# Feed-forwards of a two-block transformer: the third gate/up piece computed by seven block products, like the pieces behind it

## The chip, the cores and the metric

One core of a Trainium2 chip runs the whole program as one kernel launch. Its engines are named as the profile names them: PE multiplies matrices (PEld is its loading of weights), DVE and ACT work elementwise, POOL issues some loads and does a few copies, SP issues the other loads. The metric is the device time of one execution in microseconds; less is better.

## The reference

A first block (mixer and a mixture of experts) is followed by two layers of a second block. Each of these layers has two gated feed-forwards with a mixer between them, so there are four feed-forwards, and the change lies in them alone. All arithmetic is float32.

```python
def swiglu_2(h, w_gu, w_down):
    gu = h @ w_gu
    g, u = jnp.split(gu, 2, axis=-1)
    return (jax.nn.silu(g) * u) @ w_down
...
    for l in range(DEPTH_2):
        h = modulate(x, g_norm[l, 0], mod[:, 0], mod[:, 1])
        x = x + 0.5 * mod[:, 2][:, None, :] * swiglu_2(h, w_ffn1_gu[l], w_ffn1_down[l])
        ...
        x = x + 0.5 * mod[:, 8][:, None, :] * swiglu_2(h, w_ffn2_gu[l], w_ffn2_down[l])
```

There are 512 tokens, 1024 features and 2816 hidden units.

## The kernel before

`gated_layer` is one feed-forward. Activations lie with features on the partitions, so `h` is 8 tiles of 128 features by 512 tokens. A float32 product is made of three passes over parts of a lower precision (`mm3`, lines 470 to 475): weights and activations are each split into a high part (ACT copies them rounded) and a low part (DVE subtracts), and PE adds high by high, high by low and low by high.

The gate/up half goes over 22 pieces (`FT`). A piece is the weights of 128 hidden units, gate and up, for all 1024 features: 2048 values in a partition, 1 MB, in four quarters of 512 that stand for gate or up and for one half of the features. Two kinds of piece exist:

- A plain piece (`first()` for piece 0, `plain(n)` for the others): SP loads the whole piece (L166), ACT makes the high part (L173), DVE the low part (L178), PE does 48 matmuls of 512 tokens, ACT the silu (L712), DVE the product with up (L862). Before the change pieces 0, 1 and 2 are plain (`PLAIN = 3`).
- A piece by seven block products (`seven_products`): features, tokens and gate/up are halved, and seven products of blocks take the place of eight. Each is 12 matmuls of 256 tokens, 84 for a piece, in the order one, two, four (on the unchanged weight quarters, the "pure" ones), six, seventh, five, three (on sums of quarters). The products four, six, seventh and five use sums of the activations, T (`t_high`, `t_low`), made once in a stage: DVE lines 944 to 952, ACT L753, DVE L958. For the weights SP loads three quarters (L576, 0.75 MB), and POOL makes two sums over quarters by loads alone: L835 loads one quarter twice into `pair_raw`, and when that has landed L837 loads two other quarters with the addition done by the transfer. DVE adds two more sums (L876, L878). Then come the splits: ACT L735 and DVE L868 for the pure quarters, ACT L741 and DVE L883 for the pair, ACT L743 and DVE L889 for the sums. L889 increments `low_done`, which says that the weights of the piece are ready.

Raw weights, `pair_raw` and the split weights have two places each, for even and odd pieces. So `low_done` of piece n lets SP issue the load of piece n + 2 and POOL issue L835 of piece n + 2. POOL goes in order of pieces: L835, wait for its landing, L837, then the next piece. A piece that is written out ahead of the loop, with a number below `PLAIN + 2`, has no such wait: before the change that is piece 3 alone, and L835 of piece 4 waits for the low part of piece 2 (L178).

The results of the products are put together by DVE from PSUM: `first_rows` (L897, L899) when product six is done, `middle_rows` (L905) when ACT has kept product five (L728), `last_rows` (L913, L916) when product three is done, then ACT's silu (L717) and `finish` (L922). ACT keeps product one of the next piece (L724, `kept`) behind that silu. In the order written for DVE, the work of piece n stands between that of piece n + 1:

```python
(before or last_rows)(*((r, 0) if s else (r - 1, 1)))
split_pure(*behind)
if not before:
    finish(*((r, 0) if s else (r - 1, 1)))
make_sums(*behind)
split_pair(*behind)
first_rows(r, s)
split_sums(*behind)
middle_rows(r, s)
```

PE's product two of piece n waits for `first_rows` of piece n - 1 (they share a PSUM bank), product four of the first such piece waits for T (`t_ready`), and product six of piece n waits for `low_done` of piece n and for `kept` of piece n.

In PSUM the plain pieces use banks 0 and 1, 6 and 7, 0 and 1; the seven products of even pieces use banks 0 to 2 (by place, see `half_bank`) and of odd ones banks 3 to 5, and both a half of bank 6. Behind the 22 pieces comes the down half: 11 loads of 1 MB, plain matmuls, and in three of the four feed-forwards also the next layers' modulation (DVE L131).

Of the kernel before, what the change touches and what calls it, by code (L numbers as in the profile page):

```python
# [24 lines left out]
S = 512  # L25
# [13 lines left out]
FT = 22  # L39


PLAIN = 3
LATE = 8
# [367 lines left out]
class Kernel:  # L411
# [82 lines left out]
    def gated_layer(self, h, parts_area, shift, gate, w_gu, w_dn, then, beside=None, late=False):  # L494
# [6 lines left out]
        with self.stage("ffn"):  # L501
# [43 lines left out]
            plain_banks = [(0, 1), (6, 7), (0, 1)]  # L545
# [21 lines left out]
            with nc.Block() as block:  # L567
                @block.sync
                def _(sp):
                    def piece(r, s):  # L570
                        return w_gu[bass.ds(2 * r + s, 1)].rearrange("a p k n -> (a p) (k n)")
# [8 lines left out]
                    w.load(sp, 2, 2, piece(1, 0))  # L580
                    up(1, 1)
                    up(2, 0)
                    up(2, 1)
                    pair_by_pair(sp, up, 6, FT)
# [22 lines left out]
                def _(pe):  # L607
# [10 lines left out]
                    def plain(n):  # L618
                        w.ready(pe, 0, n)
                        if n == 2:  # L620
                            pe.wait_ge(hid_done, 1)
                        for bank, sem in ((0, gate_ps), (1, w.used)):
                            for k in range(KD):
                                mm = mm3(ps[:, plain_banks[n][bank], :], piece_part(n, bank, k), (h[0][:, k, :], h[1][:, k, :]),
                                         start=k == 0, stop=k == KD - 1)
                            mm.then_inc(sem, 1)
# [63 lines left out]
                    for n in range(1, PLAIN):  # L690
                        plain(n)
                    if late:
                        pair_by_pair(pe, seven_products, PLAIN, LATE + 5)
                        pe.wait_ge(late_added, KD)
                        nc.tensor.matmul(ps[:, 7, :], self.ones[:], late_sum, start=True, stop=True).then_inc(late_summed, 1)
                        pair_by_pair(pe, seven_products, LATE + 5, FT)
                    else:
                        pair_by_pair(pe, seven_products, PLAIN, FT)
# [8 lines left out]
                def _(act):  # L707
# [28 lines left out]

                    def split_sums(r, s):
                        n = 2 * r + s
                        act.wait_ge(pair_summed[s], count(r, s))
                        act.wait_ge(w.used, n + (w.base - 1))  # L740
                        a(w.high[:, w.slot(s), 2 * S:4 * S], pair_raw[:, s].rearrange("p a n -> p (a n)"), ACT.Copy).then_inc(pair_high, 1)  # L741
                        act.wait_ge(sums_made, 2 * number(n) + 2)
                        a(w.high[:, w.slot(s), 0:2 * S], w.raw[:, w.slot(s), 0:2 * S], ACT.Copy).then_inc(w.high_done, 1)  # L743
                    of = lambda n: (n // 2, n % 2)
# [5 lines left out]
                    w.split_high(act, 1, 0)  # L750
# [3 lines left out]
                    plain_silu(1)  # L754
                    split_pure(*of(PLAIN))
# [3 lines left out]
                    def body(r, s, silu=None, pure=True):  # L759
# [3 lines left out]
                        keep_first(r, s)  # L763
                        split_sums(*behind)
# [43 lines left out]
                def _(pool):  # L808
# [21 lines left out]
                    def add_second(r, s):  # L830
                        n = 2 * r + s
                        first = w_gu[bass.ds(n, 1)].rearrange("a p k n -> (a p) (k n)")[:, 3 * S:4 * S]
                        if not (isinstance(n, int) and n < PLAIN + 2):
# [4 lines left out]
                                            .rearrange("p (b c n) -> p b c n", b=2, c=2)[:, :, 0], accum_op=ALU.add).then_inc(pair_summed[s], 16)  # L838
                    if late:
                        pair_by_pair(pool, add_second, PLAIN, LATE + 2)  # L840
# [5 lines left out]
                    else:  # L846
                        pair_by_pair(pool, add_second, PLAIN, FT)
# [8 lines left out]
                def _(dve):  # L856
# [80 lines left out]
                    of = lambda n: (n // 2, n % 2)  # L937
# [17 lines left out]
                    w.split_low(dve, 1, 0)  # L955
# [4 lines left out]
                    finish_plain(1)  # L960
                    split_pure(*of(PLAIN))
                    make_sums(*of(PLAIN))
                    split_pair(*of(PLAIN))
# [2522 lines left out]
```

## Time and profile before

| | |
|---|---|
| median of 3 timed runs | 2945.81 us (2941.64 to 2947.32) |
| the profiled execution | 2935.07 us, span 2933.4 us |
| PE busy | 2823.1 us, 96% of the span |
| DVE busy | 2257.0 us, 77% |
| ACT busy | 1464.7 us, 50% |
| granted TensorE clock | 0.991 of full speed |
| gate/up halves of the four feed-forwards | about 1160 to 1383, 1688 to 1909, 2043 to 2266 and 2570 to 2793 us |

The profiled execution is one execution; its own time stands 10.7 us below the median of the timed runs. An engine's idle time costs something only where PE, or whatever the end waits for, waits for it.

### The profile page before, as it was taken

The numbers are of one execution on the slowest core, as the hardware profiler recorded it, in microseconds if no ns is written. First come the engines' busy times: TensorE is split into PE (matmuls) and PEld (weight loads), VectorE is DVE, ScalarE is ACT, GpSimd is POOL, SyncE is SP. The second block draws the span as 40 slices with busy tenths as digits, with TensorE's granted clock in tenths as the row PEclk, the third lists the DMA queues.
The fourth block names the chain that finished last, engine by engine and source line by source line (L and its number), as shares of the span: only waits on it lengthen the run. The fifth ranks groups of instructions, "written<-read, shape, count | busy, mean of one in ns | idle before, by whom it ended". The sixth has DMA issues, their size and how long they took to land. (4 is left out here: it accounts for less than half of the span.)

```text
span 2933.4 us, 46960 instructions
## 1 busy us (share of the span) xinstructions
PE 2823.1 (96%) x16536; PEld 2373.6 (81%) x16536; DVE 2257.0 (77%) x2837; ACT 1464.7 (50%) x1817; POOL 472.1 (16%) x545
## 2 busy tenths in 40 slices
PE   8999798999999999999999999999999999999998
PEld 4876566777777777999877789987999877789986
DVE  7857757999999987887876588777787776587843
ACT  5125535888888884454135454423444135354422
POOL 0110002333433330131100011100111000011100
PEclk9999899999999999999999999999999999999999
DMA  8552236999999997566842156675565842156631
GB/s 325 175 202 96 90 151 236 364 361 374 375 366 359 363 354 279 160 177 168 319 163 83 58 161 174 171 285 206 150 182 157 324 164 87 58 158 175 172 113 59
DMA packets 147474, 615.47 MB, mean 210 GB/s; under 512 B 23088, under 2 KB 24624, under 8 KB 115120
## 3 DMA queue, kind: packets, MB, share of 16 engines
q1 hardware_dynamic: 89264, 471.51, 43.2%
q0 software_dynamic: 58112, 142.66, 18.0%
q8 instruction: 61, 1.00, 0.1%
q14 instruction: 37, 0.30, 0.0%
HBM read 608.87 MB, written 37.75 MB: 220 GB/s over the span
## 5 line engine op out<-in xcount | busy, mean ns | idle before, releaser
L178 DVE TENSOR_TENSOR stream_low<-stream_raw,stream_high 128x2048 fp32r<-128x2048 f32 x80 | 183.2, 2290 | 213.2 <-ACT stream_high L173 212.5
L173 ACT ACTIVATE stream_high<-stream_raw 128x2048 fp32r<-128x2048 f32 x75 | 143.4, 1914 | 386.8 <-PE ffn_ps_psum L475 317.9
L317 DVE TENSOR_TENSOR expert_low<-expert_raw,expert_high 128x2048 fp32r<-128x2048 f32 x128 | 292.5, 2285 | 4.8 <-ACT expert_high L313 2.0
L473 PE MATMUL ffn_ps_psum<-ffn_pure_high,stream_high 128*128 128x512 f32 x704 | 277.3, 394 | 0.0
L474 PE MATMUL ffn_ps_psum<-ffn_pure_low,stream_high 128*128 128x512 f32 x704 | 274.0, 389 | 0.0
L475 PE MATMUL ffn_ps_psum<-ffn_pure_high,stream_low 128*128 128x512 f32 x704 | 274.0, 389 | 0.0
L473 PE MATMUL ffn_ps_psum<-ffn_t_high,stream_high 128*128 128x256 f32 x912 | 258.7, 284 | 1.2 <-ACT area_f L724 1.2
L475 PE MATMUL ffn_ps_psum<-ffn_t_high,stream_low 128*128 128x256 f32 x912 | 258.2, 283 | 0.0
L474 PE MATMUL ffn_ps_psum<-ffn_t_low,stream_high 128*128 128x256 f32 x912 | 258.2, 283 | 0.0
L313 ACT ACTIVATE expert_high<-expert_raw 128x2048 fp32r<-128x2048 f32 x128 | 244.7, 1912 | 18.4 <-PE experts_g_psum L475 17.7
L473 PE MATMUL experts_g_psum<-expert_high,experts_xh 128*128 128x512 f32 x512 | 207.4, 405 | 14.7 <-DVE experts_xl L3221 13.0
L475 PE MATMUL experts_g_psum<-expert_high,experts_xl 128*128 128x512 f32 x512 | 201.4, 393 | 0.0
L474 PE MATMUL experts_g_psum<-expert_low,experts_xh 128*128 128x512 f32 x512 | 200.7, 392 | 0.0
L473 PEld LDWEIGHTS ffn_ps_psum<-ffn_t_high,stream_high 128*128 128x128 f32 x912 | 175.1, 192 | 2.1 <-ACT area_f L724 2.0
L475 PEld LDWEIGHTS ffn_ps_psum<-ffn_t_high,stream_low 128*128 128x128 f32 x912 | 175.1, 192 | 0.0
L474 PEld LDWEIGHTS ffn_ps_psum<-ffn_t_low,stream_high 128*128 128x128 f32 x912 | 175.1, 192 | 0.0
L473 PE MATMUL ffn_ps_psum<-h_high_f,ffn_pure_high 128*128 128x256 f32 x608 | 172.9, 284 | 0.8 <-DVE area_f L899 0.7
L475 PE MATMUL ffn_ps_psum<-h_high_f,ffn_pure_low 128*128 128x256 f32 x608 | 172.1, 283 | 0.0
L474 PE MATMUL ffn_ps_psum<-h_low_f,ffn_pure_high 128*128 128x256 f32 x608 | 172.1, 283 | 0.0
L837 POOL DMA_DIRECT2D con<-in_ffn_gu x76 | 83.1, 1093 | 522.0 <-DMA con<-in_ffn_gu 522.0
L835 POOL DMA_DIRECT2D con<-in_ffn_gu x76 | 56.5, 743 | 629.1 <-POOLq L439 475.7
L473 PEld LDWEIGHTS ffn_ps_psum<-ffn_pure_high,stream_high 128*128 128x128 f32 x704 | 132.2, 188 | 29.1 <-issue 1.9
(546 smaller groups left out, 7898.3 us busy)
## 6 DMA issues: line engine op xcount, KB each, us to landing
expert_raw<-in_exp_gu SPq DMA_DIRECT2D x128, 1024.0 KB, 8.8
con<-in_ffn_gu POOLq DMA_DIRECT2D x152, 512.0 KB, 6.2
expert_raw<-in_exp_dn SPq DMA_DIRECT2D x64, 1024.0 KB, 10.3
ffn_mod_rows<-in_w_mod SPq DMA_DIRECT2D x120, 512.0 KB, 5.2
stream_raw<-in_ffn_gu SPq DMA_DIRECT2D x76, 768.0 KB, 6.1
stream_raw<-in_ffn_dn SPq DMA_DIRECT2D x44, 1024.0 KB, 7.0
mix_mod_rows<-in_w_ada POOLq DMA_DIRECT2D x32, 512.0 KB, 4.6
stream_raw<-in_w_in SPq DMA_DIRECT2D x16, 1024.0 KB, 5.7
```

Of the source, the lines that this page charges most:

```text
L173: self.nc.scalar.activation(self.high[:, q], self.raw[:, q], ACT.Copy).then_inc(self.high_done, 1)
L178: self.nc.vector.tensor_tensor(self.low[:, q], self.raw[:, q], self.high[:, q].bitcast(F32), ALU.subtract)\
L313: nc.scalar.activation(self.high[:, j].rearrange("p k n -> p (k n)"), self.raw[:, s, j], ACT.Copy).then_inc(self.w_high, 1)
L317: nc.vector.tensor_tensor(self.low[:, j].rearrange("p k n -> p (k n)"), self.raw[:, s, j], self.high[:, j].rearrange("p k n -> p (k n)").b ...
L473: mm(out, w[0], x[0], start=start, stop=False)
L474: mm(out, w[0], x[1], start=False, stop=False)
L475: return mm(out, w[1], x[0], start=False, stop=stop)
L835: nc.gpsimd.dma_start(pair_raw[:, s], first.unsqueeze(1).broadcast_to([P, 2, S])).then_inc(pair_loaded[s], 16)
L837: nc.gpsimd.dma_start(pair_raw[:, s], w_gu[bass.ds(2 * r + s, 1)].rearrange("a p k (q n) -> (a p) (k q n)", q=2) .rearrange("p (b c n) -> ...
```

## The change

Piece 2 becomes a piece by seven products; pieces 0 and 1 stay plain. Piece 1's PSUM banks become 3 and 4. SP loads three quarters of piece 2 where it loaded the whole piece, and POOL issues L835 and L837 for piece 2 ahead of those of piece 3. On DVE the splits and sums of piece 2 stand ahead of and around the split of T: pure quarters, sums and pair ahead of it, the low part of the sums (which sets `low_done`) behind it. On ACT the pair's high part is a function of its own, `split_pair`; in the loop it is called just where it stood. PE goes from plain piece 1 to the seven products of pieces 2 and 3 and then into the loop, which starts at piece 3 or 4 on every engine as before the change or one piece earlier.

```diff
-PLAIN = 3
+PLAIN = 2
...
-            plain_banks = [(0, 1), (6, 7), (0, 1)]
+            of = lambda n: (n // 2, n % 2)
+            plain_banks = [(0, 1), (3, 4)]
...
                 @block.sync
...
-                    w.load(sp, 2, 2, piece(1, 0))
+                    up(1, 0)
                     up(1, 1)
-                    up(2, 0)
-                    up(2, 1)
-                    pair_by_pair(sp, up, 6, FT)
+                    pair_by_pair(sp, up, 4, FT)
...
                 @block.tensor
...
                         w.ready(pe, 0, n)
-                        if n == 2:
-                            pe.wait_ge(hid_done, 1)
...
                     for n in range(1, PLAIN):
                         plain(n)
+                    seven_products(*of(PLAIN))
                     if late:
-                        pair_by_pair(pe, seven_products, PLAIN, LATE + 5)
+                        pair_by_pair(pe, seven_products, PLAIN + 1, LATE + 5)
...
                     else:
-                        pair_by_pair(pe, seven_products, PLAIN, FT)
+                        pair_by_pair(pe, seven_products, PLAIN + 1, FT)
...
                 @block.scalar
...
+                    def split_pair(r, s):
+                        act.wait_ge(pair_summed[s], count(r, s))
+                        act.wait_ge(w.used, 2 * r + (s + w.base - 1))
+                        a(w.high[:, w.slot(s), 2 * S:4 * S], pair_raw[:, s].rearrange("p a n -> p (a n)"), ACT.Copy).then_inc(pair_high, 1)
+
                     def split_sums(r, s):
                         n = 2 * r + s
-                        act.wait_ge(pair_summed[s], count(r, s))
-                        act.wait_ge(w.used, n + (w.base - 1))
-                        a(w.high[:, w.slot(s), 2 * S:4 * S], pair_raw[:, s].rearrange("p a n -> p (a n)"), ACT.Copy).then_inc(pair_high, 1)
                         act.wait_ge(sums_made, 2 * number(n) + 2)
...
                     plain_silu(0)
-                    w.split_high(act, 1, 0)
+                    split_pure(*of(PLAIN))
+                    split_pair(*of(PLAIN))
                     for i, src in enumerate((first_k, second_k)):
                         act.wait_ge(t_made, 2 + 2 * i)
                         a(t_high[:, 4 * i:4 * i + 4, :], src, ACT.Copy).then_inc(t_split, 1)
-                    plain_silu(1)
-                    split_pure(*of(PLAIN))
                     split_sums(*of(PLAIN))
                     split_pure(*of(PLAIN + 1))
...
                         keep_first(r, s)
+                        split_pair(*behind)
                         split_sums(*behind)
...
                 @block.gpsimd
...
+                    add_second(*of(PLAIN))
+                    add_second(*of(PLAIN + 1))
                     if late:
-                        pair_by_pair(pool, add_second, PLAIN, LATE + 2)
+                        pair_by_pair(pool, add_second, PLAIN + 2, LATE + 2)
...
                     else:
-                        pair_by_pair(pool, add_second, PLAIN, FT)
+                        pair_by_pair(pool, add_second, PLAIN + 2, FT)
...
                 @block.vector
...
                     finish_plain(0)
-                    w.split_low(dve, 1, 0)
+                    split_pure(*of(PLAIN))
+                    make_sums(*of(PLAIN))
+                    split_pair(*of(PLAIN))
                     for i, src in enumerate((first_k, second_k)):
                         dve.wait_ge(t_split, i + 1)
...
-                    finish_plain(1)
-                    split_pure(*of(PLAIN))
-                    make_sums(*of(PLAIN))
-                    split_pair(*of(PLAIN))
                     split_sums(*of(PLAIN))
```

## Rows read from the trace of the kernel before

**Rows 1.** The page: busy time, share and instructions of each engine.
```profile
PE 2823.1 (96%) x16536; PEld 2373.6 (81%) x16536; DVE 2257.0 (77%) x2837; ACT 1464.7 (50%) x1817; POOL 472.1 (16%) x545
```

**Rows 2.** Timeline of PE, first and second feed-forward: start, duration, line [idle <-releaser].
```profile
1172.92 0.50 PE L473 MATMUL ffn_ps_psum<-h_high_f,stream_high 128*128 128x512 f32 x1 [0.21 <-DVE stream_low L178]
...
1194.84 0.28 PE L473 MATMUL ffn_ps_psum<-h_high_f,ffn_pure_high 128*128 128x256 f32 x1
...
1699.71 0.39 PE L473 MATMUL ffn_ps_psum<-h_high_f,stream_high 128*128 128x512 f32 x1
...
1721.47 0.28 PE L473 MATMUL ffn_ps_psum<-h_high_f,ffn_pure_high 128*128 128x256 f32 x1
...
1731.54 0.28 PE L473 MATMUL ffn_ps_psum<-h_high_f,ffn_pure_high 128*128 128x256 f32 x1
```

**Rows 3.** Timeline of PE: first pure product of piece 3, product six of piece 21.
```profile
1382.09 0.39 PE L473 MATMUL ffn_ps_psum<-ffn_t_high,stream_high 128*128 128x256 f32 x1 [0.33 <-ACT area_f L724]
...
1908.31 0.39 PE L473 MATMUL ffn_ps_psum<-ffn_t_high,stream_high 128*128 128x256 f32 x1 [0.32 <-ACT area_f L724]
...
2078.36 0.28 PE L473 MATMUL ffn_ps_psum<-h_high_f,ffn_pure_high 128*128 128x256 f32 x1
...
2264.11 0.28 PE L473 MATMUL ffn_ps_psum<-ffn_t_high,stream_high 128*128 128x256 f32 x1
...
2603.31 0.28 PE L473 MATMUL ffn_ps_psum<-h_high_f,ffn_pure_high 128*128 128x256 f32 x1
...
2791.22 0.28 PE L473 MATMUL ffn_ps_psum<-ffn_t_high,stream_high 128*128 128x256 f32 x1
```

**Rows 4.** Timeline of DVE at the start of the first and second feed-forward.
```profile
1177.77 0.68 DVE L862 SCALAR_TENSOR_TENSOR ffn_hid<-ffn_hid,ffn_ps_psum 128x512 f32<-128x512 f32 x1
...
1702.73 0.68 DVE L862 SCALAR_TENSOR_TENSOR ffn_hid<-ffn_hid,ffn_ps_psum 128x512 f32<-128x512 f32 x1
1703.33 2.28 DVE L178 TENSOR_TENSOR stream_low<-stream_raw,stream_high 128x2048 fp32r<-128x2048 f32 x1
1705.53 4.49 DVE L958 TENSOR_TENSOR ffn_t_low<-ffn_hid,ffn_t_high 128x2048 fp32r<-128x2048 f32 x2
...
1711.40 1.75 DVE L868 TENSOR_TENSOR ffn_pure_low<-stream_raw,ffn_pure_high 128x1536 fp32r<-128x1536 f32 x1
1713.25 0.69 DVE L876 TENSOR_TENSOR stream_raw<-stream_raw,con 128x512 f32<-128x512 f32 x1
...
1715.80 1.23 DVE L889 TENSOR_TENSOR stream_low<-stream_raw,stream_high 128x1024 fp32r<-128x1024 f32 x1
```

**Rows 5.** Timeline of POOL: the loads for the pair of piece 4, second feed-forward.
```profile
1706.31 0.73 POOL L835 DMA_DIRECT2D con<-in_ffn_gu  x1 [8.80 <-DVE stream_low L178]
1712.52 1.09 POOL L837 DMA_DIRECT2D con<-in_ffn_gu  x1 [5.49 <-DMA con<-in_ffn_gu]
```

**Rows 6.** Transfers, the L837 issued at 1712.52: size, time to landing.
```profile
con<-in_ffn_gu POOLq DMA_DIRECT2D x1, 512.0 KB, 5.5
```

**Rows 7.** Timeline, fourth feed-forward, piece 18: POOL, SP, DVE and PE.
```profile
2737.39 0.73 POOL L835 DMA_DIRECT2D con<-in_ffn_gu  x1 [2.57 <-issue]
...
2744.90 1.09 POOL L837 DMA_DIRECT2D con<-in_ffn_gu  x1 [6.78 <-DMA con<-in_ffn_gu]
...
2744.97 0.33 SPq L576 DMA_DIRECT2D stream_raw<-in_ffn_gu  x1
...
2753.13 0.69 DVE L876 TENSOR_TENSOR stream_raw<-stream_raw,con 128x512 f32<-128x512 f32 x1 [4.30 <-DMA con<-in_ffn_gu]
...
2756.38 1.22 DVE L889 TENSOR_TENSOR stream_low<-stream_raw,stream_high 128x1024 fp32r<-128x1024 f32 x1
...
2759.91 0.39 PE L473 MATMUL ffn_ps_psum<-ffn_t_high,stream_high 128*128 128x256 f32 x1 [0.25 <-ACT area_f L724]
```

**Rows 8.** Timeline of DVE, fourth feed-forward: L889 of pieces 8 and 20.
```profile
2652.69 1.22 DVE L889 TENSOR_TENSOR stream_low<-stream_raw,stream_high 128x1024 fp32r<-128x1024 f32 x1
...
2777.45 1.22 DVE L889 TENSOR_TENSOR stream_low<-stream_raw,stream_high 128x1024 fp32r<-128x1024 f32 x1
```

More of the change, by code:

```diff
@@ L735, in split_pure @@
                         a(pure_h[:, s], w.raw[:, w.slot(s), 0:3 * S], ACT.Copy).then_inc(pure_high, 1)
+                    def split_pair(r, s):
+                        act.wait_ge(pair_summed[s], count(r, s))
+                        act.wait_ge(w.used, 2 * r + (s + w.base - 1))
+                        a(w.high[:, w.slot(s), 2 * S:4 * S], pair_raw[:, s].rearrange("p a n -> p (a n)"), ACT.Copy).then_inc(pair_high, 1)
                     def split_sums(r, s):
                         n = 2 * r + s
-                        act.wait_ge(pair_summed[s], count(r, s))
-                        act.wait_ge(w.used, n + (w.base - 1))
-                        a(w.high[:, w.slot(s), 2 * S:4 * S], pair_raw[:, s].rearrange("p a n -> p (a n)"), ACT.Copy).then_inc(pair_high, 1)
                         act.wait_ge(sums_made, 2 * number(n) + 2)
                         a(w.high[:, w.slot(s), 0:2 * S], w.raw[:, w.slot(s), 0:2 * S], ACT.Copy).then_inc(w.high_done, 1)
-                    of = lambda n: (n // 2, n % 2)
                     norm.scalar(act)
@@ L936, in window @@
                                 .then_inc(window_low, 1)
-                    of = lambda n: (n // 2, n % 2)
                     norm.vector(dve)
```

## Prediction

> **What bounds the kernel now.** I read the page first. PE is busy for 96% of the span and DVE for 77% [rows 1], so a stage gets shorter where PE has less to do, as long as nothing makes PE wait. Then I read the timeline of PE through the four gate/up halves. A plain piece takes 10.96 us in the first (21.92 for two) and 10.88 in the second (21.76 for two); a piece by seven products takes 10.07 [rows 2], and 10.08 over the whole third stage (2078.36 to 2264.11 for 18 pieces and 36 of the 84 matmuls of one more [rows 3]). Its 84 matmuls are thus 0.12 us apart, and product six, behind 36 of them, starts 4.32 us into the piece.
>
> Next I asked whether PE keeps that pace to piece 21. From the first product of piece 3 to product six of piece 21 it would take 18 x 10.08 + 4.32 = 185.76 us. The four stages took 187.25, 186.84, 185.75 and 187.91 [rows 2, 3]. So the third loses nothing, the others lose 1.5, 1.1 and 2.15 us, 4.7 together, and at the end of the first two the wait is for ACT's L724.
>
> Where that comes from stands in the timelines of DVE and POOL. For piece 18 of the fourth stage, L876 sat idle for 4.3 us until the load of L837 had landed. L889, which makes the piece's weights ready, started 3.25 us behind L876 and ended 4.47 behind it, and product six started 2.31 us after that end, when DVE's later rows, ACT's silu and L724 were through [rows 7]. So the chain that ends last there is a circle through the loads: L889 of piece n, L835 of piece n + 2, its landing, L837, its landing, L876, L889. It has two pieces of PE's work, 20.16 us, for one round. From piece 8 to piece 20 of that stage six rounds took 124.76 us, 20.79 each [rows 8], and the last one 21.07 [rows 7, 8]: the loads are slower than PE. They cost little before because they start with a lead and lose it late.
>
> The time of L837 varies. Issued at 1712.52, with nothing beside it at first, it landed after 5.5 us [rows 5, 6]. Issued within 0.1 us of SP's load of the next piece (2744.90 and 2744.97), it landed after 8.2 [rows 7].
>
> **The change part by part.**
>
> *PE.* It removes 48 matmuls of 512 tokens and adds 84 of 256 in each stage: 10.96 - 10.07 = 0.9 us in the first stage and 0.8 in each of the others, 3.3 us in all. This is all that can be gained directly, 0.11% of the time.
>
> *DVE at the start of a stage.* Gone is the low part of piece 2 (L178, 2.28 us) ahead of T's. Added are L868, L876, L878 and L883 ahead of it, and L889 behind it. L868 to L889 took 4.40 us from start to start, and the two halves of T's low part 4.41 (1711.40 to 1715.80; 4.49 less the overlap at the end) [rows 4]. In the second stage L862 starts at 1702.73 and takes 0.60, so L889 of piece 2 starts at 1702.73 + 0.60 + 4.40 + 4.41 = 1712.14 and ends at 1713.36. Before, the low part of piece 2 ended at 1705.61: the signal that frees the places for piece 4 comes 7.75 us later, and it is what SP's load and L835 of piece 4 wait for. I price that under the loads.
>
> *PE's first wait.* Product four of piece 2 wants T's low part, which ends at 1712.2 in the second stage. PE is there at 1699.71 + 10.88 + 24 x 0.12 = 1713.47: no wait. In the first stage DVE is later, since it also splits piece 1 there: L862 at 1177.77 gives an end at 1187.26, and PE is there at 1172.92 + 10.96 + 2.88 = 1186.76. That costs 0.5 us.
>
> *SP and POOL.* Piece 2's own loads are hidden: SP brings 0.75 MB for 1 MB, POOL's L835 and L837 start with the stage, where those of piece 3 stood, and those of piece 3 queue behind them; DVE gets to L876 of piece 2 at 1705.19 and to that of piece 3 at 1715.8, and the norm and plain piece 0 cover the time until then. If that cover were gone, L876 would be late by what the loads overrun. ACT's work is the same in kind and has idle time; the pair's high part in the loop stands where it stood.
>
> *The loads for piece 4 and on.* In the second stage L889 of piece 2 ends at 1713.36. L835 follows after 0.70 (1705.61 to 1706.31 [rows 4, 5]), L837 6.21 us later, at 1720.27. Meanwhile DVE does piece 3: L862 0.60, L868 1.85, L876 to L889 3.25, L889 1.22, together 6.92, so L889 of piece 3 ends at 1720.28 and SP loads piece 5 just then. That is the case of [rows 7], the two issued within 0.1 us of each other, so L837 lands after 8.2 us, at 1728.5. L889 of piece 4 ends at 1732.97, and product six can start at 1735.28. PE would be there at 1710.59 (1699.71 + 10.88) + 20.16 + 4.32 = 1735.07. So PE waits from the first round on, by 0.2 us here. The third and fourth stages start like the second. In the first, L889 of piece 2 ends at 1177.77 + 0.60 + 4.40 + 4.41 + 1.22 = 1188.40, the round of 19.6 us puts product six of piece 4 at 1210.3, and PE is there at 1183.88 + 0.5 + 20.16 + 4.32 = 1208.9: 1.4 us. With the 0.5 above, the four starts cost 0.5 + 1.4 + 3 x 0.2 = 2.5 us.
>
> The Trainium skill's page "DMA: Bandwidth & Descriptors", section "Anatomy of one DMA — SWDGE (gpsimd) path", fits a load like L835 or L837 by 2.0 us plus its bytes over 436 GB/s; for 512 KB that is an estimate of 3.2 us. With it a round would be some 12 us, no stage would lose anything, and the sum would be the first rival's below. The rows disagree, 5.5 us alone and 8.2 beside another load [rows 6, 7], and I go by them.
>
> From piece 4 to piece 20 come eight more rounds in each stage. No trace shows a whole stage in that state. The nearest rows are the six late rounds of the fourth stage, 20.79 each, and the last of them, with PE waiting, 21.07. I take the middle, 20.93, because PE waited in the last rounds only: 0.77 us over 20.16, 6.2 in a stage, 24.6 in four.
>
> The losses that the kernel had, 4.7 us, are the same kind and are replaced. **Sum:** 24.6 + 2.5 - 4.7 - 3.3 = 19.1 us more. The profiled execution would take 2935.07 + 19.1 = 2954 us. It stood 10.7 us below the median of the runs shown, so for a median I add the 19.1 to 2945.8: **2965 us**, 0.65% more.
>
> *Bounds of the round.* If only half of the rounds are long (the fourth stage took until piece 8 to fall behind), it is 12.3 for 24.6: 7 us more, 2953. If L835 is slowed like L837, to 8.2, a round is 0.70 + 8.2 + 8.2 + 4.47 = 21.57, 1.41 too many, 45 in all: 40 us more, 2985.
>
> **The rivals.**
>
> *The loads stay hidden* (as the page's estimate has it). L837 of piece 4 lands after 5.5 us for 8.2, because SP's load falls a little later than I have it. Then L889 of piece 4 ends 2.7 us earlier, PE doesn't wait, and the lead grows again. For it speaks the third stage, which ran 18 pieces without loss; against it that my walk puts the two issues 0.01 us apart, and that the fourth stage lost 6 x 0.63 = 3.8 us of its lead in six rounds, more than these 2.5. It gives the gain of PE less the 0.5: 2.8 us less, 2943, within the bound of 0.2% (5.9 us), which is about what a measurement of this kernel can tell from no change. It is also the case in which the change does next to nothing.
>
> *Faster.* The place of SP's load relative to L837 decides whether a stage falls behind. If the new phase keeps them apart in all stages, as in the third one now, the 4.7 us go as well: 3.3 + 4.7 - 0.5 = 7.5 us less, 2938. It decides from the point where L837 lands within some 6 us in each round. Against it speaks the same 0.01 us.
>
> *Both loads slow from the start*, the upper bound above: 2985. For it speaks that L835 and L837 then never have the transfers to themselves; against it the 7.5 us from L835 to L837 in a late round [rows 7], where both were in flight.
>
> **How the numbers follow.** The forecast has 0.74, with 2953 to 2985 as its own range; the loads hidden 0.17, faster 0.04, both slow 0.05. Slower by over 0.2% is 0.74 + 0.05 = 0.79, within it 0.17, faster 0.04. The range goes from just below the hidden case, 2942, to 2981, short of the upper bound, since that needs every round at its worst: eight rounds at 21.07, the longest that the rows show, are 0.91 x 32 = 29.1 and give 24 us more, 2969. Outside remain the faster rival, the one with both loads slow, and the topmost part of the forecast's range, some 0.12.
>
> **What would show it.** Right: each stage has one plain piece behind piece 0; L835 of piece 4 is released by L889; the even pieces' L876 idles for the load from piece 4 on, some 8 us behind L837; L889 to L889 of even pieces is near 21 us; PE waits some 0.8 us in a round, at products two and six. Wrong: the even pieces' L837 lands in less than 6 us and PE's pieces stay 10.08 us apart to piece 21; or PE's wait for `t_ready`, or one for the pure quarters of piece 2, is well over the 0.5 us here; or the down half takes back what the gate/up half lost.

## The result, and the profile after

The changed kernel takes 2963.7 us (median of 6 runs, 2955.86 to 2972.45) and the kernel before, run beside it, 2943.35 us (6 runs, 2932.41 to 2947.32). The ratio is 1.0076, with a 95% interval from 1.0058 to 1.0094: the change costs some 22 us. The forecast was 2965 us with a range from 2942 to 2981.

The profiled execution took 2960.48 us, 25.4 more than the one before. The page of the changed kernel: busy time of each engine, the matmuls on T and the sums (among them product six's first), those of products one and two, and L877 (L876 before; many lines are off by one or two in the changed file: L834 and L836 are the pair's loads, L890 was L889, L722 was L724).

```profile
PE 2836.1 (96%) x16680; PEld 2386.9 (81%) x16680; DVE 2278.2 (77%) x2873; ACT 1470.7 (50%) x1833; POOL 481.7 (16%) x553
...
L473 PE MATMUL ffn_ps_psum<-ffn_t_high,stream_high 128*128 128x256 f32 x960 | 274.5, 286 | 6.9 <-ACT area_f L722 6.7
...
L473 PE MATMUL ffn_ps_psum<-h_high_f,ffn_pure_high 128*128 128x256 f32 x640 | 183.6, 287 | 6.0 <-DVE area_f L900 5.8
...
L877 DVE TENSOR_TENSOR stream_raw<-stream_raw,con 128x512 f32<-128x512 f32 x80 | 55.1, 688 | 139.0 <-DMA con<-in_ffn_gu 138.1
```

There are 144 more matmuls, as the diff says, four times 84 less 48 [rows 1]. L877 sat idle for 138.1 us behind the pair's loads; before it was 58. PE's idle time shows only part of the loss: 6.9 us, nearly all ahead of product six, and 6.0 ahead of product two. PE's busy time also rose, by 13.0 us, though it has 3.2 us less to do.

So I measured each gate/up half from the first matmul of plain piece 1 to the first matmul of the down half. Two of these pairs in the timeline of PE of the changed kernel, second and fourth feed-forward:

```profile
1714.44 0.39 PE L473 MATMUL ffn_ps_psum<-h_high_f,stream_high 128*128 128x512 f32 x1
...
1932.73 0.40 PE L473 MATMUL ffn_ps_psum<-ffn_pure_high,stream_high 128*128 128x512 f32 x1
...
2605.03 0.39 PE L473 MATMUL ffn_ps_psum<-h_high_f,stream_high 128*128 128x512 f32 x1
...
2822.39 0.40 PE L473 MATMUL ffn_ps_psum<-ffn_pure_high,stream_high 128*128 128x512 f32 x1
```

They are 218.29 and 217.36 us apart. Where PE never waits the stretch takes 212.47 us with the change and 213.27 without it (the first and second experiment below show both, three stages each, equal to 0.01 us). What is above that is called waiting here:

| gate/up half of stage | 1 | 2 | 3 | 4 | sum |
|---|---|---|---|---|---|
| before, us | 215.03 | 214.45 | 213.27 | 215.42 | |
| of it waiting | 1.8 | 1.2 | 0.0 | 2.2 | 5.1 |
| after, us | 222.72 | 218.29 | 218.16 | 217.36 | |
| of it waiting | 10.3 | 5.8 | 5.7 | 4.9 | 26.7 |

The four halves are 18.4 us longer: 21.6 of waiting more, 3.2 of matmuls less. Some 1.5 us of the third stage's 5.7 are not a wait. They follow PE's longest wait in the four halves, ahead of product two of piece 6: the matmuls behind it are 0.21 us apart for 0.12, at a granted clock of 0.50, the lower of its two levels (1.2 GHz). The rows are that wait in PE's timeline, and then PE's windows behind it and ahead of it (from:to, us, PE busy and matmuls, granted clock, DMA share, GB/s):

```profile
2128.30 0.39 PE L473 MATMUL ffn_ps_psum<-h_high_f,ffn_pure_high 128*128 128x256 f32 x1 [1.75 <-DVE area_f L900]
```
```profile
2129.00:2132.00 3.00, 3.00 (x16) 0.50 1.04 212
2121.00:2124.00 3.00, 3.00 (x28) 1.00 1.01 272
```

The other 7 of the 25.4 us lie ahead of the first feed-forward, whose first pair load was issued at 1160.43 before and at 1167.48 after. Nothing was changed there, and that point moved between 1165.27 and 1176.68 in the experiments: it is a difference between executions.

How a stage begins, in the timelines of the second feed-forward: piece 2's first product; L890 of piece 2; the loads for piece 4; L890 of piece 3; SP's load of piece 5; L877 and L890 of piece 4; product six of piece 4.

```profile
1725.32 0.28 PE L473 MATMUL ffn_ps_psum<-h_high_f,ffn_pure_high 128*128 128x256 f32 x1
...
1726.79 1.22 DVE L890 TENSOR_TENSOR stream_low<-stream_raw,stream_high 128x1024 fp32r<-128x1024 f32 x1
...
1728.69 0.73 POOL L834 DMA_DIRECT2D con<-in_ffn_gu  x1 [9.99 <-DVE stream_low L890]
...
1733.62 1.22 DVE L890 TENSOR_TENSOR stream_low<-stream_raw,stream_high 128x1024 fp32r<-128x1024 f32 x1
...
1734.85 1.09 POOL L836 DMA_DIRECT2D con<-in_ffn_gu  x1 [5.43 <-DMA con<-in_ffn_gu]
...
1735.02 0.34 SPq L577 DMA_DIRECT2D stream_raw<-in_ffn_gu  x1
...
1744.15 0.69 DVE L877 TENSOR_TENSOR stream_raw<-stream_raw,con 128x512 f32<-128x512 f32 x1 [5.07 <-DMA con<-in_ffn_gu]
...
1747.40 1.22 DVE L890 TENSOR_TENSOR stream_low<-stream_raw,stream_high 128x1024 fp32r<-128x1024 f32 x1
...
1750.93 0.39 PE L473 MATMUL ffn_ps_psum<-ffn_t_high,stream_high 128*128 128x256 f32 x1 [0.25 <-ACT area_f L722]
```

L890 of piece 2 ends 2.69 us after the piece's first product and releases L834 of piece 4. L836 follows 6.16 us later, SP's load 0.17 behind that, and the pair is complete only at 1744.13. Without a wait product six would start at 1725.32 + 20.16 + 4.32 = 1749.80; it starts 1.13 later, in the first round.

The same chain, rounds later, in the fourth feed-forward. The first six rows are piece 8's round: L890 of piece 6, both loads, SP's load, L877, L890 of piece 8. The rest is piece 19's, from L890 of piece 17 to product six, with L890 of piece 18 between.

```profile
2657.75 1.22 DVE L890 TENSOR_TENSOR stream_low<-stream_raw,stream_high 128x1024 fp32r<-128x1024 f32 x1
...
2659.64 0.73 POOL L834 DMA_DIRECT2D con<-in_ffn_gu  x1 [2.20 <-DVE stream_low L890]
...
2666.07 1.09 POOL L836 DMA_DIRECT2D con<-in_ffn_gu  x1 [5.71 <-DMA con<-in_ffn_gu]
...
2667.59 0.33 SPq L577 DMA_DIRECT2D stream_raw<-in_ffn_gu  x1
...
2672.14 0.69 DVE L877 TENSOR_TENSOR stream_raw<-stream_raw,con 128x512 f32<-128x512 f32 x1 [0.68 <-DMA con<-in_ffn_gu]
...
2675.39 1.22 DVE L890 TENSOR_TENSOR stream_low<-stream_raw,stream_high 128x1024 fp32r<-128x1024 f32 x1
...
2770.72 1.22 DVE L890 TENSOR_TENSOR stream_low<-stream_raw,stream_high 128x1024 fp32r<-128x1024 f32 x1
...
2772.62 0.73 POOL L834 DMA_DIRECT2D con<-in_ffn_gu  x1 [2.24 <-DVE stream_low L890]
...
2779.15 1.22 DVE L890 TENSOR_TENSOR stream_low<-stream_raw,stream_high 128x1024 fp32r<-128x1024 f32 x1
...
2780.13 1.09 POOL L836 DMA_DIRECT2D con<-in_ffn_gu  x1 [6.79 <-DMA con<-in_ffn_gu]
...
2780.54 0.33 SPq L577 DMA_DIRECT2D stream_raw<-in_ffn_gu  x1
...
2788.55 0.69 DVE L877 TENSOR_TENSOR stream_raw<-stream_raw,con 128x512 f32<-128x512 f32 x1 [4.13 <-DMA con<-in_ffn_gu]
...
2791.81 1.22 DVE L890 TENSOR_TENSOR stream_low<-stream_raw,stream_high 128x1024 fp32r<-128x1024 f32 x1
...
2795.33 0.38 PE L473 MATMUL ffn_ps_psum<-ffn_t_high,stream_high 128*128 128x256 f32 x1 [0.26 <-ACT area_f L722]
```

These rows show how the state keeps itself up. L890 of a late piece is followed by that of the next one 8.43 us later (2770.72 to 2779.15), as fast as DVE can, where pieces on time are 10.08 apart. That second L890 releases SP's load, so the load falls 0.41 us behind the late chain's next L836, which then takes 8.4 us. The result is the next late L890, 21.09 us after the last (2770.72 to 2791.81), where PE's work takes 20.16. When L834 lands a little earlier, L836 leaves further ahead of SP's load (1.52 us for piece 8), lands after 6.0, and the round takes 17.64 us (2657.75 to 2675.39); afterwards the odd pieces took over the late place. The view of transfers of the changed kernel for those three L836, at 1734.85, 2666.07 and 2780.13 (size, us from issue to landing):

```profile
con<-in_ffn_gu POOLq DMA_DIRECT2D x1, 512.0 KB, 9.3
...
con<-in_ffn_gu POOLq DMA_DIRECT2D x1, 512.0 KB, 6.0
...
con<-in_ffn_gu POOLq DMA_DIRECT2D x1, 512.0 KB, 8.4
```

Over the loads L836 of pieces 4 to 21 of all stages, 72 of them, 34 had an SP load issued between 0.4 us before and 1.1 us after: they took 8.50 us in the mean (7.97 to 10.03; for piece 21 in two stages, that load is the down half's first). The other 38 took 5.87 (5.58 to 7.29). Before there were 18 of the first kind and 54 of the second.

### The profile page after: what moved, and what is told of

Its sections match the earlier page's. It is cut to its first block and busy times, and to the rows that moved or that the text cites. A ratio compares the mean times of both kernels' runs of the same rounds, so it can differ in the third digit from the quotient of the medians.

```text
span 2958.9 us, 47391 instructions
## 1 busy us (share of the span) xinstructions
PE 2836.1 (96%) x16680; PEld 2386.9 (81%) x16680; DVE 2278.2 (77%) x2873; ACT 1470.7 (50%) x1833; POOL 481.7 (16%) x553
## 5 line engine op out<-in xcount | busy, mean ns | idle before, releaser
L178 DVE TENSOR_TENSOR stream_low<-stream_raw,stream_high 128x2048 fp32r<-128x2048 f32 x76 | 174.1, 2291 | 213.1 <-ACT stream_high L173 212.7
L473 PE MATMUL ffn_ps_psum<-ffn_t_high,stream_high 128*128 128x256 f32 x960 | 274.5, 286 | 6.9 <-ACT area_f L722 6.7
L475 PE MATMUL ffn_ps_psum<-ffn_t_high,stream_low 128*128 128x256 f32 x960 | 271.7, 283 | 0.0
L474 PE MATMUL ffn_ps_psum<-ffn_t_low,stream_high 128*128 128x256 f32 x960 | 271.6, 283 | 0.0
L738 ACT ACTIVATE stream_high<-con 128x1024 fp32r<-128x1024 f32 x80 | 84.8, 1060 | 238.4 <-DMA con<-in_ffn_gu 238.4
L473 PE MATMUL ffn_ps_psum<-h_high_f,ffn_pure_high 128*128 128x256 f32 x640 | 183.6, 287 | 6.0 <-DVE area_f L900 5.8
L474 PE MATMUL ffn_ps_psum<-h_low_f,ffn_pure_high 128*128 128x256 f32 x640 | 181.4, 284 | 0.0
L475 PE MATMUL ffn_ps_psum<-h_high_f,ffn_pure_low 128*128 128x256 f32 x640 | 181.4, 283 | 0.0
L836 POOL DMA_DIRECT2D con<-in_ffn_gu x80 | 87.5, 1093 | 574.5 <-DMA con<-in_ffn_gu 568.8
L877 DVE TENSOR_TENSOR stream_raw<-stream_raw,con 128x512 f32<-128x512 f32 x80 | 55.1, 688 | 139.0 <-DMA con<-in_ffn_gu 138.1
```

Of the source, the lines that this page charges most:

```text
L178: self.nc.vector.tensor_tensor(self.low[:, q], self.raw[:, q], self.high[:, q].bitcast(F32), ALU.subtract)\
L473: mm(out, w[0], x[0], start=start, stop=False)
L474: mm(out, w[0], x[1], start=False, stop=False)
L475: return mm(out, w[1], x[0], start=False, stop=stop)
L836: nc.gpsimd.dma_start(pair_raw[:, s], w_gu[bass.ds(2 * r + s, 1)].rearrange("a p k (q n) -> (a p) (k q n)", q=2) .rearrange("p (b c n) -> ...
L877: v.tensor_tensor(a11, a11, pair_raw[:, s, 1], ALU.add).then_inc(sums_made, 1)
```

## The experiments

Theory: the change makes each stage start late, and a late chain keeps SP's load beside the accumulating load, which costs it 2.6 us and so a longer round than PE's. Rivals: there is simply more to load; DVE has more to do; the third piece by seven products is itself dearer, T needed earlier included.

All were timed beside the kernel before. "Waiting" is that of the four gate/up halves in one profiled execution, against 212.47 or 213.27 us as the third piece is; "beside" counts the 72 loads as above. The profiled executions of kernels 3 and 9 were the fastest of their runs (2939.44 us for a median of 2949.82, and 2953.18 for 2964.48), so their waiting reads low. The count alone does not set the waiting: 3 and 9 have 22 each.

| kernel | ratio to before, 95% | waiting, us | beside |
|---|---|---|---|
| before | 1 | 5.1 | 18 |
| the change | 1.0076, 1.0058 to 1.0094 | 26.7 | 34 |
| 1 change, SP's load behind the pair | 0.9992, 0.9974 to 1.0009 | 2.1 | 0 |
| 2 before, SP's load behind the pair | 0.9988, 0.9974 to 1.0001 | 1.0 | 0 |
| 3 change, piece 2's sums ahead of T | 1.0023, 1.0009 to 1.0037 | 9.0 | 22 |
| 4 change, pair of piece 4 early | 1.0006, 0.9993 to 1.0019 | 6.4 | 18 |
| 5 change, 1 and 4 together | 0.9988, 0.9976 to 1.0001 | 1.5 | 0 |
| 6 before, late load of piece 5 | 1.0045, 1.0030 to 1.0060 | 14.7 | 27 |
| 7 before, 6 and 2 together | 0.9989, 0.9976 to 1.0002 | 1.0 | 0 |
| 8 before, late load of piece 6 | 1.0056, 1.0037 to 1.0076 | 20.6 | 24 |
| 9 before, late loads of 5 and 6 | 1.0079, 1.0059 to 1.0099 | 19.9 | 22 |

**1 and 2: SP's load held back.** In the changed kernel and in the one before, SP waits until the pair of piece n - 1 has landed before it loads piece n.

```diff
                         sp.wait_ge(w.low_done, n + (w.base - 1))
+                        if not (isinstance(n, int) and n < 4):
+                            before = (r, 0) if s else (r - 1, 1)
+                            sp.wait_ge(pair_summed[before[1]], count(*before))
                         sp.dma_start(w.raw[:, w.slot(s), 0:3 * S], src[:, 0:3 * S])
```

> The changed kernel, with one thing more: from piece 4 on SP's load of piece n also waits until the pair of piece n - 1 has landed, so that it can't run beside L837's transfer of that piece. Theory (the circle of loads is too long because SP's load stretches L837's transfer): the even pieces' accumulating load lands in 5.5 to 6.5 us for 8.4, a round of the circle fits into 20.16 us, PE waits only the 0.5 us of the first stage's start, and the losses of the kernel before go too: 3.3 + 4.7 - 0.5 = 7.5 us below the kernel before, ratio about 0.9975. Rival 1 (the third piece's extra 0.75 MB in a stage, or the transfers' total, sets the pace): the same bytes move, so it stays near 1.0076. Rival 2 (DVE is late: its added work ahead of and around T's split): stays near 1.0076 too.

> The kernel before, with the same extra wait of SP. Theory: its own 4.7 us of late rounds go and nothing else, ratio about 0.998; the distance to the changed kernel with this wait is what PE saves by the seven products, 3.3 - 0.5 = 2.8 us, 0.1%. Rivals 1 and 2: 1.000, since the kernel before is not late at the start of a stage.

The loss is gone: 0.9992 for 1.0076, with the same bytes, the same matmuls and the same work on DVE. A round of piece 17 in the fourth stage of the first kernel, between PE's first and last point of that half: the accumulating load (L840 here, L836 in the change), SP's load, L881 (L877) and L894 (L890).

```profile
2587.11 0.39 PE L473 MATMUL ffn_ps_psum<-h_high_f,stream_high 128*128 128x512 f32 x1
...
2734.91 1.09 POOL L840 DMA_DIRECT2D con<-in_ffn_gu  x1 [6.07 <-DMA con<-in_ffn_gu]
...
2740.71 0.33 SPq L580 DMA_DIRECT2D stream_raw<-in_ffn_gu  x1
...
2742.75 0.68 DVE L881 TENSOR_TENSOR stream_raw<-stream_raw,con 128x512 f32<-128x512 f32 x1
2746.00 1.22 DVE L894 TENSOR_TENSOR stream_low<-stream_raw,stream_high 128x1024 fp32r<-128x1024 f32 x1
...
2799.58 0.40 PE L473 MATMUL ffn_ps_psum<-ffn_pure_high,stream_high 128*128 128x512 f32 x1
```

L840 takes 5.7 us (the view of transfers), SP's load leaves 5.80 us behind it, and L881 no longer waits. The half takes 212.47 us. In the kernel before the same wait gives 213.27 in three stages, so the change is worth 0.80 us of matmuls a stage. Against before, the first kernel's four halves are 6.2 us shorter (851.9 for 858.2), but from the first feed-forward's first pair load to the end of the execution it gained only 3.0 us (1769.95 for 1772.94), and timed 2.4 (0.9992, with 1 in the interval), where 7.5 were expected. The rest went in the mixers behind stages 1 and 3. PE's windows of the first kernel, at the head of the second of these mixers (from:to, us, PE busy and matmuls, granted clock, DMA share, GB/s), and of the same place before:

```profile
2404.20:2405.90 1.70, 1.70 (x6) 0.50 1.02 429
```
```profile
2400.20:2401.90 1.70, 1.70 (x9) 1.00 0.90 371
```

Eight matmuls are 0.43 us apart there, at the lower of the two clocks (1.2 GHz), and 0.23 before: 1.6 us in each mixer. Before them PE has a pause of 1.49 us for the norm in both kernels. The slow stretch goes with the wait: in the four kernels that hold SP's load back (1, 2, 5, 7), seven of the eight mixers behind stages 1 and 3 have it, and in the seven other kernels none of the 14 has it at this place. So what the wait gains in the halves is in part lost there. Why the clock is lower was not found.

**3 and 4: the start made earlier.** The third kernel splits piece 2's sums ahead of T on ACT and DVE, so that L890 of piece 2 is earlier and T's low part later. The fourth loads the pair of piece 4 early, into two free tiles of `hid`.

```diff
                     split_pair(*of(PLAIN))
+                    split_sums(*of(PLAIN))
                     for i, src in enumerate((first_k, second_k)):
...
-                    split_sums(*of(PLAIN))
```
```diff
+            pair_of = lambda r, s: hid[:, 9:11, :] if isinstance(r, int) and (r, s) == (2, 0) else pair_raw[:, s]
...
-                        if not (isinstance(n, int) and n < PLAIN + 2):
+                        if not (isinstance(n, int) and n < PLAIN + 3):
                             pool.wait_ge(w.low_done, n + (w.base - 1))
-                        nc.gpsimd.dma_start(pair_raw[:, s], first.unsqueeze(1).broadcast_to([P, 2, S])).then_inc(pair_loaded[s], 16)
+                        nc.gpsimd.dma_start(pair_of(r, s), first.unsqueeze(1).broadcast_to([P, 2, S])).then_inc(pair_loaded[s], 16)
```

> The changed kernel, with the split of piece 2's sums moved ahead of the split of T on ACT and DVE; all work and all bytes stay. Theory: L889 of piece 2 ends 4.4 us earlier, so L837 of piece 4 is issued some 5 us ahead of SP's load of piece 5 and lands in under 6.5 us; the stages start with a lead of about 3 us, as those of the kernel before did, and lose it late or never: 0 to 2.5 us in a stage, T's split costs up to 1.5 us more in the first, ratio 0.998 to 1.002. Rivals 1 and 2 (bytes, or DVE's amount of work): no change in either, so it stays near 1.0076.

> The changed kernel, with the pair of piece 4 loaded to a free place of its own (two tiles of the hidden activations that are written only with pieces 9 and 10), so that its two POOL loads follow those of piece 3 at once and wait for nothing; SP's loads stay as they are. Theory: L876 of piece 4 doesn't wait, L889 of piece 4 is some 3 us ahead of what PE needs, and the circle starts with that lead: losses of 0 to 2.5 us in a stage as in the kernel before, ratio 0.998 to 1.002. Rivals 1 and 2: near 1.0076. If SP's load beside L837 costs a lead of 3 us within a few rounds whatever the start, it lies between, at 1.003 to 1.006.

Both recover most of the loss without any wait on SP, at 1.0023 (3) and 1.0006 (4); kernel 3 lies just above the range expected, 0.998 to 1.002. Half of its waiting, 4.5 of 9.0 us, is not for loads: product four of piece 2 waits for T's low part, which is now later. PE is held up there by 2.4 us in the first stage and by 0.7 in each of the others (PE's timeline of kernel 3, first stage; L961 makes T's low part; it is L960 in the change):

```profile
1194.39 0.39 PE L473 MATMUL ffn_ps_psum<-ffn_t_high,ffn_pure_high 128*128 128x256 f32 x1 [2.16 <-DVE ffn_t_low L961]
```

Neither cures every stage: stages still fall behind later, as they do in the kernel before, and 22 and 18 loads still lie beside SP's. In the fourth stage of kernel 4 none does, and the half takes 212.47.

**5: both cures.**

> The kernel after with both earlier cures: the ordinary load of piece n (from 4 on) waits until the pair of piece n - 1 is summed, and the pair of piece 4 is loaded early into two free hid tiles. My theory: with the first cure alone no round is late any more, and what is left is about 2 us in the first feed-forward (T ready 0.5 us late, and some late sums of the first pieces); the early pair can take away at most the 1.5 us of late sums, so this kernel is the one with the first cure alone or 1 us below it: ratio to before 0.997 to 0.999. Rival: the two cures add up (each gained some 15 us and more against the kernel after); then the time would fall by over 10 us below before, ratio under 0.996.

0.9988: the cures don't add up. With SP's load held back there is almost nothing left to take.

**6 and 7: only the start made late, in the kernel before.** The third piece stays ordinary, and POOL waits once in each stage.

```diff
+                    for n in (PLAIN, PLAIN + 1):
+                        add_second(n // 2, n % 2)
+                    pool.wait_ge(products, 3)
                     if late:
-                        pair_by_pair(pool, add_second, PLAIN, LATE + 2)
+                        pair_by_pair(pool, add_second, PLAIN + 2, LATE + 2)
```

> The kernel before, with its ordinary third piece, and one wait added for each feed-forward: GpSimd issues the pair load of piece 5 only after three products of piece 3 (about 4.4 us after that piece's first product, some 7.8 us later than before; the kernel after issues the one of piece 4 some 5.1 us after piece 2's first product). No work, no bytes and no order on any other engine is changed. My theory: the late start alone, kept up by the accumulating load that the ordinary load stretches, makes the loss; so this kernel loses about what the change lost in its stages, without the 0.8 us that the change saves on the matmuls: 3.5 to 6 us in each of the four stages, 14 to 20 us in all, ratio 1.0045 to 1.007. Rival: the loss belongs to the third piece itself (its products, its sums, T needed earlier), and the two pieces of room are enough to recover from one late load; then the ratio is 0.999 to 1.001.

> The same late load in the kernel before, and the wait of the first cure with it: the ordinary load of piece n (from 6 on) waits until the pair of piece n - 1 is summed. My theory: a load that lies alone takes 5.5 to 5.9 us, so a round takes 17.5 to 18 us of work where 20.16 are to be had, and the 7.8 us are won back within four rounds without a wait of TensorE above 1 us: ratio 0.998 to 1.000, as the kernel before with that wait alone. Rival, that a late start by itself is what costs: the same ratio as the late load without the wait, 1.0045 to 1.007.

One late load in each stage, and nothing else, costs 0.45%, some 13 us. With SP's load held back as well, the same late load costs nothing (0.9989). DVE's timeline in the first stage of kernel 7 (L883 is L877 in the change, pieces 5 to 8), with POOL's late load:

```profile
1207.95 0.73 POOL L839 DMA_DIRECT2D con<-in_ffn_gu  x1 [23.98 <-PE ffn_ps_psum L475]
...
1219.16 0.69 DVE L883 TENSOR_TENSOR stream_raw<-stream_raw,con 128x512 f32<-128x512 f32 x1 [2.18 <-DMA con<-in_ffn_gu]
...
1229.77 0.69 DVE L883 TENSOR_TENSOR stream_raw<-stream_raw,con 128x512 f32<-128x512 f32 x1 [0.81 <-DMA con<-in_ffn_gu]
...
1238.96 0.69 DVE L883 TENSOR_TENSOR stream_raw<-stream_raw,con 128x512 f32<-128x512 f32 x1
...
1247.40 0.69 DVE L883 TENSOR_TENSOR stream_raw<-stream_raw,con 128x512 f32<-128x512 f32 x1
```

From piece 7 on L883 no longer waits: lateness is worked off when SP's load is held back. The delay in 6 and 7 is of the kind that the change makes, not of its size. The pair load of piece 5 leaves 4.78 us behind the first product of piece 3 in every stage, and in the change that of piece 4 leaves 5.1, 3.4, 3.3 and 1.8 us behind the first product of piece 2.

**8 and 9: where the other half is.** The single late load gave 13 of the 22 us, or of 25.6 with the 3.2 that PE saves. In the change the even piece 4 is the first late one, and both pieces of its pair start late. Kernel 8 delays piece 6 alone, kernel 9 pieces 5 and 6.

```diff
+                    pool.wait_ge(products, 3)
+                    add_second((PLAIN + 2) // 2, (PLAIN + 2) % 2)
+                    pool.wait_ge(products, 9)
```

> The kernel before, with one wait for each feed-forward as in the kernel with the late load of piece 5, but one piece on: GpSimd issues the pair load of piece 6 only after three products of piece 4, some 4.8 us after that piece's first product and 6.1 us later than before. The late load of piece 5 cost 13 us, the change 22 us and 25.6 us without what TensorE saves. The changed kernel is late at an even piece first (4), the earlier experiment at an odd one (5), and the loops of the engines jump back behind each odd piece. Theory that the place in the pair matters: this kernel loses clearly more than the 13 us, 20 to 26 us, ratio 1.007 to 1.009. Rival, that one late load gives about half of the loss wherever it falls: ratio 1.003 to 1.006, a little under the one for piece 5 since it is late by 1.7 us less.

> The kernel before with both waits: the pair load of piece 5 after three products of piece 3, and that of piece 6 after three products of piece 4. In the changed kernel both pieces of the first pair start without lead. Theory that what the single late load lacks is the second late piece: then this one loses about what the change lost without its saving on TensorE, 20 to 26 us, ratio 1.007 to 1.009. Rival, that a second late load adds nothing, since the piece behind a late one follows it 8.45 us later whatever its own load does: as with the one for piece 5, ratio 1.003 to 1.006.

With two late loads the kernel before loses 0.79%, 23 us, as much as the change. Its second load is later than the change's, though: it leaves 5.3 to 5.4 us behind the first product of piece 4, and the change's pair load of piece 5 leaves between 1.4 ahead of the first product of piece 3 and 1.7 behind it. So the equal loss does not show that an equal lateness makes it. The second stage of kernel 9, with the loads of pieces 5 and 6 behind PE, SP's load, and L881 and product six of piece 6:

```profile
1732.88 0.73 POOL L835 DMA_DIRECT2D con<-in_ffn_gu  x1 [21.09 <-PE ffn_ps_psum L475]
...
1743.52 0.73 POOL L835 DMA_DIRECT2D con<-in_ffn_gu  x1 [4.26 <-PE ffn_ps_psum L475]
...
1748.95 0.34 SPq L576 DMA_DIRECT2D stream_raw<-in_ffn_gu  x1
1749.08 1.09 POOL L837 DMA_DIRECT2D con<-in_ffn_gu  x1 [4.83 <-DMA con<-in_ffn_gu]
...
1757.24 0.69 DVE L881 TENSOR_TENSOR stream_raw<-stream_raw,con 128x512 f32<-128x512 f32 x1 [4.41 <-DMA con<-in_ffn_gu]
...
1764.02 0.39 PE L473 MATMUL ffn_ps_psum<-ffn_t_high,stream_high 128*128 128x256 f32 x1 [0.26 <-ACT area_f L724]
```

From the first late round on it is the picture of the change. Whether the place in the pair matters stays open: the interval of kernel 8 reaches into the bounds of both theories. So does how far the second late load adds to the first: the intervals of 6 and 9 just touch, and in single profiled executions one stage of a kernel loses 2.8 us and another 9.3 (kernel 9), since a round whose loads happen to leave far enough apart, as piece 8's above, can set a stage back on time. In the first stage of kernel 9 seven rounds in a row took 20.05 to 20.33 us.

Kernels 1, 2, 5 and 7 all lie at 0.9988 to 0.9992, every interval with 1 in it. They beat the change clearly; that any beats the kernel before was not shown.

## Why the prediction was right, point by point

- *PE saves 3.3 us.* Measured 0.80 in each of three stages (212.47 against 213.27), so 3.2 in all if the first stage, where PE waits in every kernel, saves as much. Right.
- *L890 of piece 2, and with it the loads of piece 4, come late.* The walk had that L890 end 2.77 us behind the piece's first product, L834 0.70 later, L836 after another 6.21, L889 of piece 3 6.92 behind that of piece 2, and SP's load within 0.01 us. Measured: 2.69, 0.68, 6.16, 6.83 and 0.17. Right. That this lateness is the cause was shown by 3 and 4, which take it away, and by kernels 6 and 9, which add nothing but lateness, though more of it than the change does.
- *L836 takes 8.2 us there.* It took 9.28, and product six of piece 4 was 1.13 us late instead of 0.2. This was the term sized too low. The first stage's start was priced at 0.5 + 1.4 = 1.9; product six of its piece 4 was 1.87 late. That the third and fourth stages start like the second was wrong: L836 took 8.13 and 9.28 us there, but product six was late by 0.05 and by nothing. In the fourth, L890 of piece 2 ended 1.09 us behind the piece's first product instead of 2.69. The four starts cost 3.05 us for 2.5.
- *Eight rounds of 20.93 in each stage.* From L890 of piece 4 to that of piece 20 the mean round took 21.17, 20.73, 20.50 and 20.47 us in the four stages. That reads low for the last two, where the late place went over to the odd pieces. By PE, product six of piece 20 was later than that of piece 4 by 8.1, 4.6, 5.0 and 3.8 us: 21.6 for the 24.6, or 0.67 us in a round for 0.77. It is not an even loss: single rounds run from 17.64 to 22.67 us, which the middle of two late rows could not show. In the third stage one round, with an L836 of 10.03 us, made PE 3.5 us late (1.5 of it the low clock), and the next eight pieces lost nothing. The first stage loses more than forecast (10.3 us of waiting for 8.1), the fourth less (4.9 for 6.4); why the first has the longest rounds was not tried.
- *The sum.* Waiting 26.7 for 24.6 + 2.5 = 27.1; old losses 5.1 for 4.7; 18.4 us more in the stages for 19.1. That it is this close is luck in part: the starts cost 0.5 us more and the rounds 3.0 less than priced, and behind product six of piece 20, where the prediction has nothing, PE lost some 1.9.
- *The old losses are of the same kind.* Kernel 2 holds SP's load back in the kernel before, and they are gone in all stages but for 1.0 us in the first. Right.
- *The rivals.* The loads stayed hidden where SP's load was held back (1, 5, 7) and in single stages elsewhere (the fourth of kernel 4). The faster rival would have had 7.5 us; kernel 1, which keeps the transfers apart by a wait that the change doesn't have, gained 6.2 in the halves and no measurable time. That both loads are slow from the start did not come: L834 of the late chain took 6.2 to 6.9 us in the last five late rounds of the fourth stage, not 8.2.
- *What the prediction didn't say* is why a late stage stays late. It took the rounds of the fourth stage as they were; the rows above give the reason, the 8.43 us between a late piece's L890 and the next one's, and kernels 1 and 7 bear it out.

## What to carry to other kernels

Where a circle of transfers and engine work has little room beside the bound engine, a change that only delays its first round can cost more than the work it saves. Look in the trace for what the late state does to the order of transfers: here it puts another queue's load beside the accumulating one and so keeps itself up. One wait that keeps two transfers apart, on a queue that has time, is worth trying before any work is moved.

## What the runs showed of the hardware

- The accumulating load of 512 KB has two lengths in the changed kernel: 8.50 us in the mean with an SP load issued from 0.4 us before to 1.1 us after it, and 5.87 otherwise, with little between. An SP load 1.52 us behind left it at 6.0. An SP load issued earlier and still under way can stretch it too: in kernel 7 six of the 72 loads took 7.4 to 8.3 us, with SP's issued 2.2 to 3.3 us before them. The step lies near the 1.09 us that L836 occupies POOL; that SP's load overtakes it until then is an idea that no run tested. The Trainium skill's page "DMA: Bandwidth & Descriptors", section "Queues, rings and completion order", says that a transfer engine takes turns between the queues that have work for it; that agrees with a longer transfer beside another one, and does not give the step.
- The same page of the Trainium skill, section "Anatomy of one DMA — SWDGE (gpsimd) path", gives an estimate of 3.2 us for these bytes by its fit. The shortest of the 72 loads took 5.58 us, so the measurement decides.
- A late stage can come back by itself: the stages of one execution of kernel 6, with the same late load in each, waited 7.3, 2.8, 4.4 and 0.2 us.
- The granted clock of PE fell to 0.50 behind a wait of 1.75 us within a gate/up half, in one of the 44 halves profiled, and cost some 1.5 us. Behind the wait of 2.16 us in kernel 3 it stayed at 1.00.
